# A hybrid encoder step whose down passes start with two interleaved products

## The chip, the cores and the metric

The kernel runs on one core of one Trainium2 chip. The metric is the device time of one execution in microseconds. TensorE (PE) does the matrix products, VectorE (DVE) and ScalarE (ACT) the element work, GpSimd (POOL) a few sums and some loads, and SyncE (SP) issues most loads and all stores.

## What is computed

One layer of a streaming encoder on 576 tokens (512 prompt frames and 64 sample frames), width 1024:

```
h = x + 1/2 * SwiGLU_1(RMSNorm(x))          # 1024 -> 2816 -> 1024
u = RMSNorm(h); q, k, v = split(u @ w_in)   # rotary on q and k
o = [sliding-window attention with sinks, differential attention] (u)
h = h + o @ w_out
h = h + 1/2 * SwiGLU_2(RMSNorm(h))
y = RMSNorm(h)
swiglu(x) = (silu(x @ wg) * (x @ wu)) @ wd
```

All of it is float32. The new keys and values are outputs too. The change touches only the two SwiGLU blocks, called FFN here.

## The kernel before

**Numbers in two parts.** Each operand is held as a high part (a copy rounded to a shorter float format, made by ACT) and a low part (the rest, made by DVE with a subtraction). A product of two such operands is three matmuls: high by high, high by low, low by high. Tiles are named `w_hi`, `w_lo` (weights), `c_hi`, `c_lo` (FFN input) and `h_hi`, `h_lo` (hidden activations). Making `w_lo` is what the code calls `lo_...`; making `w_hi` is `hi_...`.

**Periods.** After the first five hidden tiles of an FFN, the work goes in 28 periods, numbered p = 0 to 27. A period multiplies a 2 by 2 arrangement of blocks with seven products instead of eight (the Winograd form of Strassen's scheme), called P1, P5, P6, P2, P7, P3, P4 in the order in which PE runs them. A period of kind `st` makes one gate and one up tile of the hidden layer from the FFN input; a period of kind `sd` makes two output tiles of a down pass. The down projection is done in three passes, over the hidden tiles 0 to 7 (periods 4 to 7), 8 to 15 (periods 16 to 19) and 16 to 21 (periods 25 to 27, the first of which is called `BRIDGE`). So a down pass starts in the middle of the `st` periods, as soon as its hidden tiles are there. A product has 12 matmuls (4 k-tiles by 3), and 9 in the third pass.

**Banks.** P1, P6, P7 and P4 of a period sum up in one PSUM bank (A), P5 and P3 in another (C), P2 in a third (B). Partial sums are needed on their way, so ACT copies a bank out after P1, P5, P6 and P7 ("snapshots", `snap`, line 1436, into the tile `comb`). The next product that adds into that bank waits for the copy: P6 waits for the snapshot of P1, P3 for that of P5, P7 for that of P6, P4 for that of P7. PE waits for the weights as well: P6 and P3 need `lo_sums`, which is DVE's subtraction for two of the seven weight blocks.

**The order on the engines.** Everything is written out by hand, and every engine runs its instructions in that order; semaphores tie them. In an `st` period DVE takes the result out of the banks at the end with `take_c22` (line 1989, tile `side`) and `take_c1` (line 1998, tile `gate`, counted by the semaphore `g_out`). At the start of the next period ACT applies the silu to that `gate` (line 1364, waits for `g_out`), and only then takes that period's snapshots. `hidden` on DVE multiplies gate by up.

**Where a down pass starts.** The first period of a down pass needs the hidden tiles of the pass. Those of the last one or two are made shortly before: DVE's `pair_lo_a` (line 1898, tile `h_lo`) is the last, and PE's P1 waits for it before its last k-tile (semaphore `h_ready`).

**The last periods.** In periods 25 to 27 the output tiles are finished one by one. ACT makes the next stage's input from them (`next_hi`, line 1344, tile `u_hi`, in the first FFN only) and their squares (`next_square`, line 1564), POOL adds the squares (line 2431) and DVE makes the low part (`next_u`, line 1819). `add_first` and `add_second` on DVE (lines 2011 to 2029) add the products into the residual `res`. After the first FFN PE goes on with the projections and then with the sum over features of the squares (line 839), which waits for POOL's last addition.

Of the kernel before, what the change touches and what calls it, by code (L numbers as in the profile page):

```python
# [25 lines left out]
P = 128  # L26
# [3 lines left out]
HALF = TOK // 2  # L30
# [4 lines left out]
KF = D_FF // P  # L35
PLAIN = 5
PAIRED = 8
TAIL_FROM = 2 * PAIRED
TAIL = KF - TAIL_FROM
KH = KD // 2  # L40
# [10 lines left out]
PART = KH * P  # L51
PARTS = 7
# [41 lines left out]
def k_tiles(p):  # L94

    return TAIL // 2 if p >= BRIDGE else KH
# [77 lines left out]
def h_count(ffn, e, f):  # L174

    return len(H_EVENTS) * ffn + H_EVENTS.index((e, f)) + 1
# [5 lines left out]
def pair_slot(f, slot):  # L182

    if f < TAIL_FROM:
        return PARTS * (f % PAIRED // 2) + slot
    return (PARTS + 1) * ((f - TAIL_FROM) // 2) + slot + (slot >= B21)
# [203 lines left out]
def hybrid_step(nc, a, o):  # L390

    stack = ExitStack()
    with stack:
# [9 lines left out]
        w_hi = sb("w_hi", [P, PARTS * PART], FP32R)  # L403
# [219 lines left out]
        def side_of(p):  # L623

            return (p + 1) % 2
# [193 lines left out]
        def _(pe):  # L819
# [73 lines left out]
                else:  # L893
                    pe.wait_ge(d_second if n == P1 else d_first, sd_count(ffn, *former[1:]) + 1)

            def period_products(ffn, p):

                key = period_key(ffn, p)
                group, snaps = GROUP[key], 4 * (N_PERIODS * ffn + p)
                for n, (banks, c, slot) in enumerate(PRODUCTS):  # L900

                    pe.wait_ge(split_ready, group + {P1: 1, P5: 2, P6: 3, P2: 1, P7: 2, P3: 3, P4: 4}[n])
                    wait_period_banks(ffn, p, n)
                    if n in (P6, P7, P3, P4):

                        pe.wait_ge(snapped, snaps + {P6: 1, P3: 2, P7: 3, P4: 4}[n])
                    for k in range(k_tiles(p)):
                        if p == 0:
                            pe.wait_ge(c_ready, KH * ffn + k + 1)
                        elif key[0] == "sd" and key[3] == 0:  # L910
                            f = PAIRED * key[2] + 2 * k + 1
                            if f == KF - 1:
                                if n in (P1, P5):

                                    pe.wait_ge(h_ready, h_count(ffn, *(("E", f - 1) if n == P1 else ("A", f))))
                            elif n == P1:
                                pe.wait_ge(h_ready, max(h_count(ffn, "A", f), h_count(ffn, "B", f)))
                        if key[0] == "st":
                            x_hi, x_lo = c_hi[:, k, c, :], c_lo[:, k, c, :]
                        else:  # L920
                            at = pair_slot(PAIRED * key[2] + 2 * k, slot)
                            x_hi, x_lo = pair_hi[:, at, :], pair_lo[:, at, :]
                        col = n * PART + k * P
                        for e, (w_part, x_part) in enumerate(((w_hi, x_hi), (w_hi, x_lo), (w_lo, x_hi))):
                            m = nc.tensor.matmul(acc[:, banks[side_of(p)], 0:HALF], w_part[:, col:col + P],  # L925
                                                 x_part, start=n in (P1, P5, P2) and k == 0 and e == 0,
                                                 stop=k == k_tiles(p) - 1 and e == 2, skip_group_check=True)
                    m.then_inc(block_used, 1)

            def down_products(ffn, d, k, token_halves=(0, 1)):  # L930

# [342 lines left out]
        def _(act):  # L1274
# [227 lines left out]
            def late_period(ffn_no, p):  # L1502

                last = p == N_PERIODS - 1
                done = FINISHED[p]
                hi_a22(ffn_no, p)
                if p == BRIDGE:
                    hi_down(ffn_no, KD - 1, 0)
                    hi_down(ffn_no, KD - 1, 1)
                elif ffn_no == 0:  # L1510
                    next_hi(ffn_no, done[0])
                snap(snap_g[:, p % 2, 0, :], ffn_no, p, P1)
                if p > BRIDGE:
                    next_square(ffn_no, done[0])
                snap(snap_u[:, 1, :], ffn_no, p, P5)
                if ffn_no == 0:
                    next_hi(ffn_no, done[-1])
                snap(snap_g[:, p % 2, 1, :], ffn_no, p, P6)
                next_square(ffn_no, done[-1])
                if not last:  # L1520
                    hi_a1(ffn_no, p + 1)
                elif ffn_no == 0:
                    hi_block(("qk", 0))
                snap(snap_u[:, 0, :], ffn_no, p, P7)
                if not last:
                    hi_loaded_sums(ffn_no, p + 1)
                    hi_sums(ffn_no, p + 1)
# [22 lines left out]
            def next_hi(ffn_no, i):  # L1550

                wait_finished(ffn_no, i)
                u_hi_part(1, ORDER[i])
# [199 lines left out]
        def _(dve):  # L1753
# [278 lines left out]
            def period(ffn_no, p):  # L2032

                former = PERIODS[p - 1] if p else ("st", PLAIN - 1)
                f = former[1] if former[0] == "st" else None
                if p == 0:
                    pair_lo_b(ffn_no, PLAIN - 2)
                    lo_sums(ffn_no, p)
                    up_out(ffn_no, PLAIN - 1)
                if p >= 2 and PERIODS[p - 2][0] == "st" and PERIODS[p - 2][1] in ONE_LATER:  # L2040
                    pair_lo_a(ffn_no, PERIODS[p - 2][1])
                lo_a22(ffn_no, p)
                if f is None:
                    add_second(ffn_no, p - 1)
                else:
                    hidden(ffn_no, f)
                weight_sums(ffn_no, p + 1)
                if p == BRIDGE - 1:
                    pair_lo_e(ffn_no, KF - 2)
                    lo_down(ffn_no, KD - 2, 0)  # L2050
                    take_c22(ffn_no, p)
                    take_c1(ffn_no, p)
                    lo_down(ffn_no, KD - 2, 1)
                    lo_a1(ffn_no, p + 1)
                    hidden(ffn_no, KF - 1)
                    pair_lo_b(ffn_no, KF - 1)
                    lo_loaded_sums(ffn_no, p + 1)
                    pair_lo_a(ffn_no, KF - 1)
                    lo_sums(ffn_no, p + 1)
                    return  # L2060
                if f is not None and f % 2:
                    pair_lo_b(ffn_no, f)
                lo_a1(ffn_no, p + 1)
                lo_loaded_sums(ffn_no, p + 1)
                if f in (PAIRED - 1, TAIL_FROM - 1):
                    pair_lo_a(ffn_no, f)
                if PERIODS[p][0] == "st":
                    take_c22(ffn_no, p)
                    take_c1(ffn_no, p)
                else:  # L2070
                    for step in range(3):
                        add_first(ffn_no, p, step)
                lo_sums(ffn_no, p + 1)

            def late_period(ffn_no, p):

# [575 lines left out]
```

## Time and profile before

| what | value |
|---|---|
| median of 3 runs | 1053.2 us (1052.46 to 1053.62) |
| span of the profiled execution, first to last instruction | 1050.4 us |
| PE busy | 1034.0 us, 98% |
| DVE busy | 805.4 us, 77% |
| ACT busy | 561.3 us, 53% |
| POOL busy | 167.3 us, 16% |
| mean granted clock of PE | 0.996 of full speed |
| matmuls of the periods (line 925) | 4,578 of 7,644 |

The profile gives the span of its execution; its time as the runs count it is not given apart, and the median of the runs lies 2.8 us above the span. PE's busy time counts overlapping matmuls once, so a gap of PE shows best in the distance between the starts of two matmuls.

### The profile page before, as it was taken

How to read it: one execution, taken by the hardware profiler on the slowest of the kernel's cores; microseconds unless marked ns; L12 is line 12 of the kernel's file. 1: busy time of each engine (PE TensorE's matmuls, PEld its weight loads, DVE VectorE, ACT ScalarE, POOL GpSimd, SP SyncE). 2: the span in 40 equal slices, each digit the busy share in tenths (PEclk: the TensorE clock that was granted, in tenths of full speed). 3: DMA queues.
4: the chain of work that ended last, by engine and by line, in shares of the span. 5: the costliest groups of instructions: out<-in, count | busy, mean ns of one | idle time of the engine just before them, and what ended most of it. 6: DMA issues, size and time to landing. Idle time of an engine off the chain costs nothing. (4 is left out here: it accounts for less than half of the span.)

```text
span 1050.4 us, 19614 instructions
## 1 busy us (share of the span) xinstructions
PE 1034.0 (98%) x7644; PEld 1001.7 (95%) x7644; DVE 805.4 (77%) x1259; ACT 561.3 (53%) x971; POOL 167.3 (16%) x296
## 2 busy tenths in 40 slices
PE   9999999999999999999999999999999999999996
PEld 9999999999999999988888889999999999999995
DVE  6998777788778994377757865798877788778894
ACT  7535644665546663344335544544654566555663
POOL 0000000000000055032444202200000000000023
PEclk9999999999999999999999999999999999999998
DMA  5435666566675435120112212416656666666532
GB/s 207 128 96 155 182 158 182 154 161 168 164 180 172 123 91 201 61 95 21 51 51 71 76 41 80 121 41 169 186 148 161 169 164 168 178 151 171 161 84 90
DMA packets 38506, 137.33 MB, mean 131 GB/s; under 512 B 4688, under 2 KB 8272, under 8 KB 38288
## 3 DMA queue, kind: packets, MB, share of 16 engines
q1 hardware_dynamic: 30352, 107.52, 29.8%
q0 software_dynamic: 8064, 28.58, 16.8%
q8 instruction: 61, 1.00, 0.4%
q14 instruction: 29, 0.24, 0.1%
HBM read 131.10 MB, written 4.98 MB: 130 GB/s over the span
## 5 line engine op out<-in xcount | busy, mean ns | idle before, releaser
L1765 DVE TENSOR_TENSOR w_lo<-raw,w_hi 128x1024 fp32r<-128x1024 f32 (+4 forms) x187 | 198.9, 1066 | 109.8 <-ACT w_hi L1280 93.4
L925 PE MATMUL acc<-c_hi,w_lo 128*128 128x288 f32 x952 | 282.0, 296 | 0.0
L925 PE MATMUL acc<-c_hi,w_hi 128*128 128x288 f32 x952 | 280.9, 295 | 0.0
L925 PE MATMUL acc<-c_lo,w_hi 128*128 128x288 f32 x952 | 277.6, 292 | 0.0
L1280 ACT ACTIVATE w_hi<-raw 128x1024 fp32r<-128x1024 f32 (+4 forms) x157 | 140.6, 897 | 80.4 <-PE acc L925 57.0
L1436 ACT ACTIVATE comb<-acc 128x288 f32<-128x288 f32 x224 | 92.1, 411 | 166.9 <-PE acc L925 164.6
L925 PEld LDWEIGHTS acc<-c_lo,w_hi 128*128 128x128 f32 x952 | 180.8, 190 | 0.0
L925 PEld LDWEIGHTS acc<-c_hi,w_hi 128*128 128x128 f32 x952 | 179.1, 188 | 0.0
L925 PEld LDWEIGHTS acc<-c_hi,w_lo 128*128 128x128 f32 x952 | 178.5, 188 | 0.0
L925 PE MATMUL acc<-h_hi,w_hi 128*128 128x288 f32 x574 | 170.7, 297 | 1.9 <-DVE h_lo L1898 0.8
L925 PE MATMUL acc<-h_hi,w_lo 128*128 128x288 f32 x574 | 169.9, 296 | 0.0
L925 PE MATMUL acc<-h_lo,w_hi 128*128 128x288 f32 x574 | 167.9, 292 | 0.0
L1765 DVE TENSOR_TENSOR w_lo<-comb,w_hi 128x1024 fp32r<-128x1024 f32 (+2 forms) x86 | 101.3, 1178 | 18.2 <-ACT w_hi L1298 15.8
L925 PEld LDWEIGHTS acc<-h_hi,w_hi 128*128 128x128 f32 x574 | 107.9, 188 | 4.3 <-DVE h_lo L1898 1.7
L925 PEld LDWEIGHTS acc<-h_lo,w_hi 128*128 128x128 f32 x574 | 108.8, 190 | 0.0
L925 PEld LDWEIGHTS acc<-h_hi,w_lo 128*128 128x128 f32 x574 | 107.8, 188 | 0.0
L829 PE MATMUL acc<-h_hi,w_hi 128*128 128x288 f32 x320 | 69.3, 298 | 0.0
L829 PE MATMUL acc<-h_lo,w_hi 128*128 128x288 f32 x320 | 68.5, 295 | 0.0
L829 PE MATMUL acc<-h_hi,w_lo 128*128 128x288 f32 x320 | 68.5, 295 | 0.0
L1304 ACT ACTIVATE w_hi<-comb 128x1024 fp32r<-128x1024 f32 (+1 forms) x56 | 58.1, 1037 | 8.9 <-PE acc L925 7.5
L829 PEld LDWEIGHTS acc<-h_hi,w_hi 128*128 128x128 f32 x320 | 51.7, 188 | 0.2
L2431 POOL TENSOR_TENSOR side<-side 128x576 f32<-128x576 f32 x23 | 36.8, 1602 | 93.2 <-issue 53.0
(257 smaller groups left out, 1858.9 us busy)
## 6 DMA issues: line engine op xcount, KB each, us to landing
raw<-in_w1st SPq DMA_DIRECT2D x17, 768.0 KB, 4.3
raw<-in_w2st SPq DMA_DIRECT2D x17, 768.0 KB, 4.2
raw<-in_w_qk SPq DMA_DIRECT2D x13, 512.0 KB, 3.8
raw<-in_w1sd SPq DMA_DIRECT2D x8, 768.0 KB, 4.2
raw<-in_w2sd SPq DMA_DIRECT2D x8, 768.0 KB, 4.3
raw<-in_w1gu SPq DMA_DIRECT2D x10, 512.0 KB, 4.5
raw<-in_w2gu SPq DMA_DIRECT2D x10, 512.0 KB, 3.9
raw<-in_w1st SPq DMA_DIRECT2D x9, 512.0 KB, 5.1
```

The source lines that it names most:

```text
L829: m = nc.tensor.matmul(acc[:, bank + t, 0:HALF], w_part[:, col:col + P], x_part[:, k, t * HALF:(t + 1) * HALF], start=first and n == 0, st ...
L925: m = nc.tensor.matmul(acc[:, banks[side_of(p)], 0:HALF], w_part[:, col:col + P], x_part, start=n in (P1, P5, P2) and k == 0 and e == 0, s ...
L1280: nc.scalar.activation(cols, src, ACT.Copy).then_inc(hi_ready, 1)
L1304: nc.scalar.activation(parts_of(w_hi, P6, P3 - P6, p), w_sum[:, :, 0:width(p)], ACT.Copy).then_inc(hi_ready, 1)
L1436: nc.scalar.activation(to, acc[:, PRODUCTS[n][0][side_of(p)], 0:HALF], ACT.Copy, scale=scale).then_inc(snapped, 1)
L1765: return nc.vector.tensor_tensor(cols, src, hi.bitcast(FP32), ALU.subtract).then_inc(split_ready, 1)
L2431: nc.gpsimd.tensor_tensor(ssq[:], ssq[:], square, ALU.add).then_inc(ssq_added, 1)
```

## The change

There are three edits, all in the FFN.

**PE.** In the first period of each down pass (4, 16 and 25 of each FFN) P1 and P5 are interleaved: P1 without its last k-tile, P5 without its last two, the last of P1, the last two of P5. All other products stay whole. The loop body moved into a function of its own, `product_steps`.

**DVE.** In the period before the first two down passes (periods 3 and 15), `lo_sums` of the next period stands ahead of `take_c22` and `take_c1` instead of behind them.

**ACT.** In the last periods of the first FFN, `next_hi` stands behind a snapshot instead of ahead of it: for the first finished tile of periods 26 and 27 behind that of P1 and not ahead of it, for the last finished tile behind that of P6 and not of P5. (In periods 26 and 27 both moves apply, in the bridge the second.)

```
-            def period_products(ffn, p):
+            def product_steps(ffn, p, n, steps):
...
+                banks, c, slot = PRODUCTS[n]
+                if steps[0] == 0:
                     pe.wait_ge(split_ready, group + {P1: 1, P5: 2, P6: 3, P2: 1, P7: 2, P3: 3, P4: 4}[n])
                     wait_period_banks(ffn, p, n)
                     if n in (P6, P7, P3, P4):
                         pe.wait_ge(snapped, snaps + {P6: 1, P3: 2, P7: 3, P4: 4}[n])
...
+            def period_products(ffn, p):
+                kind, *at = PERIODS[p]
+                n_k = k_tiles(p)
+                if kind == "sd" and at[1] == 0:
+                    last = n_k - 1
+                    for n, steps in ((P1, range(last)), (P5, range(last - 1)), (P1, range(last, n_k)),
+                                     (P5, range(last - 1, n_k))):
+                        product_steps(ffn, p, n, steps)
+                    rest = range(P6, PARTS)
+                else:
+                    rest = range(PARTS)
+                for n in rest:
+                    product_steps(ffn, p, n, range(n_k))
@@ ScalarE, late_period
                 if p == BRIDGE:
                     hi_down(ffn_no, KD - 1, 0)
                     hi_down(ffn_no, KD - 1, 1)
-                elif ffn_no == 0:
-                    next_hi(ffn_no, done[0])
                 snap(snap_g[:, p % 2, 0, :], ffn_no, p, P1)
                 if p > BRIDGE:
+                    if ffn_no == 0:
+                        next_hi(ffn_no, done[0])
                     next_square(ffn_no, done[0])
                 snap(snap_u[:, 1, :], ffn_no, p, P5)
+                snap(snap_g[:, p % 2, 1, :], ffn_no, p, P6)
                 if ffn_no == 0:
                     next_hi(ffn_no, done[-1])
-                snap(snap_g[:, p % 2, 1, :], ffn_no, p, P6)
                 next_square(ffn_no, done[-1])
@@ VectorE, period
                 lo_loaded_sums(ffn_no, p + 1)
                 if f in (PAIRED - 1, TAIL_FROM - 1):
                     pair_lo_a(ffn_no, f)
+                    lo_sums(ffn_no, p + 1)
                 if PERIODS[p][0] == "st":
                     take_c22(ffn_no, p)
                     take_c1(ffn_no, p)
...
-                lo_sums(ffn_no, p + 1)
+                if f not in (PAIRED - 1, TAIL_FROM - 1):
+                    lo_sums(ffn_no, p + 1)
```

The order on DVE at the end of period 3 of the first FFN, before. Line 1898 is `pair_lo_a`, 1989 `take_c22`, 1998 `take_c1`; the first line 1765 behind them is `lo_sums` of period 4 and the second `lo_a22`.

```order
L1898 TENSOR_TENSOR h_lo<-side,h_hi 128x1440 [waits hhi_ready,q_ready]
L1989 TENSOR_TENSOR side<-comb 128x288 [waits h_ready,snapped]
L1998 TENSOR_TENSOR gate<-acc,comb 128x576 [waits h_full,block_used]
L1765 TENSOR_TENSOR w_lo<-comb,w_hi 128x2x512 [waits hi_ready]
L1765 TENSOR_TENSOR w_lo<-raw,w_hi 128x512 [waits hi_ready]
L1875 TENSOR_TENSOR side<-side,gate 128x576 [waits c21_out,h_ready,silu_done,u_out]
```

The same place after the change, where every line number of DVE is 17 higher.

```order
L1915 TENSOR_TENSOR h_lo<-side,h_hi 128x1440 [waits hhi_ready,q_ready]
L1782 TENSOR_TENSOR w_lo<-comb,w_hi 128x2x512 [waits hi_ready]
L2006 TENSOR_TENSOR side<-comb 128x288 [waits h_ready,snapped]
L2015 TENSOR_TENSOR gate<-acc,comb 128x576 [waits h_full,block_used]
L1782 TENSOR_TENSOR w_lo<-raw,w_hi 128x512 [waits hi_ready]
L1892 TENSOR_TENSOR side<-side,gate 128x576 [waits c21_out,h_ready,silu_done,u_out]
```

The subtraction into `w_lo` from `comb` went from behind the two bank sums to ahead of them; nothing else moved. ACT's order at this place is the same in both: the silu on `gate`, then the snapshots.

```order
L1445 ACTIVATE side<-acc 128x288 [waits h_full,block_used]
L1280 ACTIVATE w_hi<-raw 128x512 [waits block_used,raw_in4]
L1364 ACTIVATE gate<-gate 128x576 [waits g_out]
L1436 ACTIVATE comb<-acc 128x288 [waits block_used,g_out]
L1436 ACTIVATE comb<-acc 128x288 [waits block_used,u_out]
```

The first line 1436 is the snapshot of P1 of period 4, and it stands behind the line 1364 that waits for `g_out`.

The order on ACT in the bridge of the first FFN, before: line 1436 are snapshots (of P1, P5 and P6), 1344 is `next_hi` and 1564 `next_square`.

```order
L1320 ACTIVATE c_lo<-comb 128x256 [waits block_used,down_in]
L1436 ACTIVATE comb<-acc 128x288 [waits block_used,g_out]
L1436 ACTIVATE comb<-acc 128x288 [waits block_used,u_out]
L1344 ACTIVATE u_hi<-res,gains 128x576 [waits res_ready]
L1436 ACTIVATE comb<-acc 128x288 [waits block_used,g_out]
L1564 ACTIVATE side<-res 128x576 [waits h_ready,res_ready]
```

After the change, where ACT's numbers are 17 higher too.

```order
L1337 ACTIVATE c_lo<-comb 128x256 [waits block_used,down_in]
L1453 ACTIVATE comb<-acc 128x288 [waits block_used,g_out]
L1453 ACTIVATE comb<-acc 128x288 [waits block_used,u_out]
L1453 ACTIVATE comb<-acc 128x288 [waits block_used,g_out]
L1361 ACTIVATE u_hi<-res,gains 128x576 [waits res_ready]
L1581 ACTIVATE side<-res 128x576 [waits h_ready,res_ready]
```

The snapshot of P6 went ahead of the copy that waits for the finished tile.

## Rows read from the trace of the kernel before

**Rows 1.** The page: the span, and each engine's busy time.

```profile
span 1050.4 us, 19614 instructions
...
PE 1034.0 (98%) x7644; PEld 1001.7 (95%) x7644; DVE 805.4 (77%) x1259; ACT 561.3 (53%) x971; POOL 167.3 (16%) x296
```

**Rows 2.** PE's waits: what waited, for what: us in total, times, longest us.

```profile
PE acc L925 <- DVE h_lo L1898: 0.8, 4, 0.2
...
PE acc L925 <- ACT comb L1436: 0.8, 2, 0.4
```

**Rows 3.** The chain that ended last: start us, us, what.

```profile
767.20 129.25 PE acc L925 x975
```

**Rows 4.** Timeline, PE, first down pass of the second FFN: start us, us, engine, line, tiles.

```profile
766.70 0.29 PE L925 MATMUL acc<-h_hi,w_lo 128*128 128x288 f32 x1
...
767.20 0.40 PE L925 MATMUL acc<-h_hi,w_hi 128*128 128x288 f32 x1 [0.20 <-DVE h_lo L1898]
...
767.44 0.30 PE L925 MATMUL acc<-h_lo,w_hi 128*128 128x288 f32 x1
...
769.16 0.29 PE L925 MATMUL acc<-h_hi,w_lo 128*128 128x288 f32 x1
...
769.37 0.40 PE L925 MATMUL acc<-h_hi,w_hi 128*128 128x288 f32 x1
```

**Rows 5.** Timeline, DVE, the same stretch.

```profile
765.49 1.66 DVE L1898 TENSOR_TENSOR h_lo<-side,h_hi 128x1440 fp32r<-128x1440 f32 x1
767.06 0.45 DVE L1989 TENSOR_TENSOR side<-comb 128x288 f32<-128x288 f32 x1
767.43 0.75 DVE L1998 TENSOR_TENSOR gate<-acc,comb 128x576 f32<-128x576 f32 x1
768.10 1.21 DVE L1765 TENSOR_TENSOR w_lo<-comb,w_hi 128x1024 fp32r<-128x1024 f32 x1
769.23 0.68 DVE L1765 TENSOR_TENSOR w_lo<-raw,w_hi 128x512 fp32r<-128x512 f32 x1
```

**Rows 6.** Timeline, ACT, the same stretch.

```profile
768.22 0.69 ACT L1364 ACTIVATE gate<-gate 128x576 f32<-128x576 f32 x1 [1.07 <-DVE gate L1998]
768.81 0.39 ACT L1436 ACTIVATE comb<-acc 128x288 f32<-128x288 f32 x1
769.56 0.41 ACT L1436 ACTIVATE comb<-acc 128x288 f32<-128x288 f32 x1 [0.36 <-PE acc L925]
```

**Rows 7.** Timeline, all engines, first down pass of the first FFN.

```profile
122.64 0.40 PE L925 MATMUL acc<-h_hi,w_hi 128*128 128x288 f32 x1 [0.20 <-DVE h_lo L1898]
...
122.87 0.75 DVE L1998 TENSOR_TENSOR gate<-acc,comb 128x576 f32<-128x576 f32 x1
```

**Rows 8.** Timeline, PE and ACT, last periods of the first FFN.

```profile
364.52 0.78 ACT L1344 ACTIVATE u_hi<-res,gains 128x576 fp32r<-128x576 f32 x1 [1.09 <-DVE res L2115]
...
365.03 0.29 PE L925 MATMUL acc<-h_hi,w_lo 128*128 128x288 f32 x1
...
365.20 0.39 ACT L1436 ACTIVATE comb<-acc 128x288 f32<-128x288 f32 x1
...
365.74 0.37 PE L925 MATMUL acc<-h_hi,w_hi 128*128 128x288 f32 x1 [0.41 <-ACT comb L1436]
...
380.72 0.37 PE L925 MATMUL acc<-h_hi,w_hi 128*128 128x288 f32 x1 [0.40 <-ACT comb L1436]
```

**Rows 9.** Timeline, DVE, POOL and PE, towards the end of the first FFN.

```profile
366.07 0.75 DVE L2012 TENSOR_TENSOR res<-res,comb 128x576 f32<-128x576 f32 x1
...
374.43 1.64 POOL L2431 TENSOR_TENSOR side<-side 128x576 f32<-128x576 f32 x1 [1.02 <-ACT side L1564]
...
374.71 1.98 DVE L2012 TENSOR_TENSOR res<-res,comb 128x576 f32<-128x576 f32 x1
...
398.59 0.61 PE L839 MATMUL acc<-ones,side 128*128 128x1 f32 x4 [0.21 <-POOL side L2431]
```

**Rows 10.** Busy time by engine in a stretch: from:to, length, PE, PEld, DVE, ACT, POOL.

```profile
372.00:397.00 25.00, 24.60 (x186) 24.40 (x185) 24.82 (x29) 15.61 (x26) 10.50 (x7) 1.00 0.37 120
```

More of the change, by code:

```diff
@@ L894, in wait_period_banks @@
                     pe.wait_ge(d_second if n == P1 else d_first, sd_count(ffn, *former[1:]) + 1)
-            def period_products(ffn, p):
+            def product_steps(ffn, p, n, steps):
                 key = period_key(ffn, p)
                 group, snaps = GROUP[key], 4 * (N_PERIODS * ffn + p)
-                for n, (banks, c, slot) in enumerate(PRODUCTS):
+                banks, c, slot = PRODUCTS[n]
+                if steps[0] == 0:
                     pe.wait_ge(split_ready, group + {P1: 1, P5: 2, P6: 3, P2: 1, P7: 2, P3: 3, P4: 4}[n])
@@ L906, in period_products @@
                         pe.wait_ge(snapped, snaps + {P6: 1, P3: 2, P7: 3, P4: 4}[n])
[L907 to L927, printed above, removed]
@@ L928, in period_products @@
-                    m.then_inc(block_used, 1)
+                for k in steps:
+                    if p == 0:
+                        pe.wait_ge(c_ready, KH * ffn + k + 1)
+                    elif key[0] == "sd" and key[3] == 0 and n in (P1, P5):
+                        f = PAIRED * key[2] + 2 * k + 1
+                        if f == KF - 1:
+                            pe.wait_ge(h_ready, h_count(ffn, *(("E", f - 1) if n == P1 else ("A", f))))
+                        elif n == P1:
+                            pe.wait_ge(h_ready, max(h_count(ffn, "A", f), h_count(ffn, "B", f)))
+                    if key[0] == "st":
+                        x_hi, x_lo = c_hi[:, k, c, :], c_lo[:, k, c, :]
+                    else:
+                        at = pair_slot(PAIRED * key[2] + 2 * k, slot)
+                        x_hi, x_lo = pair_hi[:, at, :], pair_lo[:, at, :]
+                    col = n * PART + k * P
+                    for e, (w_part, x_part) in enumerate(((w_hi, x_hi), (w_hi, x_lo), (w_lo, x_hi))):
+                        m = nc.tensor.matmul(acc[:, banks[side_of(p)], 0:HALF], w_part[:, col:col + P],
+                                             x_part, start=n in (P1, P5, P2) and k == 0 and e == 0,
+                                             stop=k == k_tiles(p) - 1 and e == 2, skip_group_check=True)
@@ new lines, in product_steps @@
+                if steps[-1] == k_tiles(p) - 1:
+                    m.then_inc(block_used, 1)
+            def period_products(ffn, p):
[7 more added lines that the diff above has]
+                    rest = range(P6, PARTS)
+                else:
+                    rest = range(PARTS)
+                for n in rest:
+                    product_steps(ffn, p, n, range(n_k))
```

## The prediction

> **What bounds the kernel now.** I read the page first: PE is busy for 1034.0 of 1050.4 us [rows 1], so what PE loses is what can be won, and any delay that PE cannot make up is paid in full. The waits of PE come next, since the change moves what PE waits for. Four matmuls of the periods waited for `h_lo` and two for a snapshot in `comb` [rows 2]. The waits are short, but a wait costs more than its idle time, so the third view is the timeline of PE at these places, with the distance between starts. The chain shows what that distance is in free running: 975 matmuls in 129.25 us, 0.133 us each, with no stop from 767.20 on [rows 3]. That row says one thing more: behind the start of a down pass nothing else limits PE for 129 us, so a delay there is not made up.
>
> **A down pass's start, before.** In the second FFN the last matmul of P1's third k-tile starts at 766.70, the next one at 767.20 and the one behind it at 767.44 [rows 4]. Instead of 0.133 these distances are 0.50 and 0.24, a loss of 0.37 and 0.11: 0.48 us. The releaser is `h_lo`, which DVE makes from 765.49 on [rows 5]. There is a second, smaller loss. P5's last matmul starts at 769.16 and P6's first at 769.37 [rows 4]: 0.21, so 0.08 lost, and its restart is as long (0.40) as that of the first stall, so I add the same 0.11. Together 0.67 us at each down pass's start. The first FFN has the same picture: the restart behind `h_lo` at 122.64 and line 1998 at 122.87, 0.23 apart, as 767.20 and 767.43 are [rows 4, 5 and 7]. With the count of four [rows 2] that makes 2.7 us, and this is all that the interleaving can win.
>
> Why does P6 start at 769.37? It needs two things. One is `lo_sums`, from 768.10 for 1.21 us, so done at 769.31 [rows 5]. The other is the snapshot of P1. ACT idles for 1.07 us until `gate` is there, runs the silu at 768.22 and the snapshot of P1 at 768.81, though a product's snapshot can start 0.40 behind its last matmul (769.16 to 769.56, P5) [rows 4 and 6]. From a snapshot's start to the matmul it lets go it is 0.54 (365.20 to 365.74) [rows 8]. So the snapshot alone would allow P6 at 769.35. The two conditions end together, within 0.02 us.
>
> **Interleaving, at the first two passes.** P1's last k-tile moves behind six matmuls of P5, to 0.133 x 7 = 0.93 us behind 766.70, so 767.63. `h_lo` allowed it at 767.20: the wait is gone. P6 then would like to start 16 distances behind 766.70, at 768.82. What is late next is P6's pair of conditions.
>
> **The swap on DVE.** Behind `pair_lo_a` DVE is free at 767.06. Now `lo_sums` runs first, for 1.13 us (768.10 to 769.23, start to start), then line 1989 at 768.19 for 0.37, then line 1998 at 768.56 instead of 767.43 [rows 5]. One condition of P6, the weights, is met at 768.27, in good time. The other is not: the silu starts 0.79 behind line 1998 (767.43 to 768.22), the snapshot of P1 0.59 behind the silu (768.22 to 768.81) [rows 5 and 6], P6 0.54 behind the snapshot. 768.56 + 0.79 + 0.59 + 0.54 = 770.48. Against 768.82 that is a stall of 1.66 us, and 0.11 for the restart: 1.77 us. Before it was 0.67. Each of the four starts costs 1.10 us more: +4.4 us. P5's snapshot follows at once and P3 is 36 matmuls on; DVE's own line 1875 behind the silu slips from 769.84 to about 770.0, and nobody needs it soon. The bounds of this term: nothing less than the 1.10 by these rows unless the snapshot runs ahead of the silu, which the order excludes; 0.2 more or less at each for the latencies, so 3.6 to 5.2.
>
> **Interleaving, at the third pass.** PE shows no wait there to be won. P1's end moves back by three matmuls, 0.40 us, and 7 distances (0.93) are left to P6. The snapshot needs 0.40 to start and 0.54 to release: 0.94. I take 0.05 us for each of the two bridges, 0.1 in all; bounds 0 and 0.4 (a restart of 0.11 and as much waiting, twice).
>
> **The copies on ACT, in the first FFN.** In the bridge ACT waits 1.09 us for `res`, runs `next_hi` at 364.52 and the snapshot of P6 at 365.20. PE's starts are 365.03 and 365.74, 0.71 apart: 0.58 lost and a restart of 0.1 [rows 8]. With the snapshot ahead this stall goes, and likewise the one at 380.72 (0.40 idle, against 0.41): 1.4 us by PE's rows alone. But this is not what sets the end of the FFN. From 372 to 397 DVE is busy for 24.82 of 25.00 us [rows 10], in an order that the change leaves alone, and PE then stops at 398.59 for the last of POOL's sums of squares [rows 9], which come from tiles that DVE finishes. A PE that is 1.4 us early waits 1.4 us there. What counts is how much earlier DVE and POOL are, and for that only the copies' own shift of some tenths speaks. I take 0.2 us won. Bounds: 1.4 won if the wait at 398.59 moves with PE; 1.2 lost if the new order puts an addition of POOL in front of a DVE instruction that PE needs (line 2012 takes 0.75 us alone, and 1.98 when POOL's addition has just started at 374.43) [rows 9].
>
> The Trainium skill bears on this (page "SBUF — State Buffer", section "Who interferes with whom"): a VectorE instruction with two SBUF inputs and a GpSimd instruction that reads SBUF exclude each other for the whole instruction. The 1.98 us agree: POOL's 1.64 from 374.43 end at 376.07, and 0.62 of DVE's time lies behind. By this rule DVE's stretch is a fixed sum of its own work and POOL's eight additions, and the term would be 0; by PE's rows alone it would be -1.4.
>
> **The sum.** 4.4 + 0.1 - 0.2 = +4.3 us on the profiled span, 1050.4 to 1054.7. The median of the runs lies 2.8 us above the span, so 1053.2 + 4.3 = 1057.5 us. A change of 0.2% (2.1 us) is what a measurement of this kernel can tell from none.
>
> **The rivals.**
>
> The wait goes and nothing takes its place (faster). P6 starts at 768.82 at all four places. It decides on line 1998: for 768.82 it would have to start at 768.82 - 1.92 = 766.90, and it started at 767.43 before `lo_sums` stood ahead of it. For it: the weights, which the trace names as releaser, are early now. Against it: ACT's 1.07 us of idle time ahead of the silu, and the order. Price: -2.7 and the copies' -0.2 to -1.4: 1050.3 to 1049.1. Chance 0.06.
>
> The edits do not do what they say (same). Were the swap without effect, P6 would start at 769.37 as before, and only one of two restarts would be saved: 4 x 0.11 = 0.4, with the copies 0.6: 1052.6. It would need a silu that is not held up by line 1998. Chance 0.07.
>
> The delay is given back at the end of the first FFN. Two of the four delays, 2.2 us, come ahead of the stretch in which PE waits for DVE and POOL; if that stretch hung on transfers alone, PE would only wait less. For it: DVE's 24.82 of 25.00. Against it: DVE's work there starts from PE's products and from splits that PE's pace sets. 1057.5 - 2.2 = 1055.3. Chance 0.06.
>
> The copies collide (slower still). POOL's additions meet other DVE instructions, and one that PE needs is held for 1.2 us: 1057.5 + 0.2 + 1.2 = 1058.9. Rows 9 show that it happens to instructions there; against it, none of them stopped PE before. Chance 0.09.
>
> **How the numbers follow.** My forecast has 0.72. Its own range is 3.6 to 5.2 for the four starts, 0 to 0.4 for the bridges and -1.4 to +0.2 for the copies; not all ends meet, so 1056.0 to 1058.5. The range for 8 in 10 reaches down to where the delay is given back and up to the collision: 1054.9 to 1059.0. Slower holds the forecast and the two cases beside it, less a remainder for cases that mix: 0.85. Same 0.08, faster 0.07.
>
> **What would show it.** In the changed kernel's waits of PE, `h_lo` is gone and four waits for `comb` of about 1.3 us or more stand at P6 of periods 4 and 16, with a distance between starts near 1.8 us. On ACT the silu there has an idle time of about 2.2 us for `gate` (1.07 before), and the snapshot follows it 0.59 later. The starts at 365.74 and 380.72 lose their wait, and the one at 398.59 grows. The prediction is wrong if P6 of period 4 starts less than 3.0 us behind the last matmul of P1's third k-tile (3.78 forecast, 2.67 before), or if the sum at line 839 shows no longer wait than before.

## The result, and the profile after

| | before | after |
|---|---|---|
| median | 1053.07 us (1052.25 to 1053.62, 6 runs) | 1060.18 us (1057.04 to 1061.81, 6 runs) |
| span of the profiled execution | 1050.4 us | 1058.0 us |
| mean granted clock in it | 0.996 | 0.992 |

The ratio is 1.0066 with an interval of 1.0056 to 1.0077: slower, as forecast, but by 7.1 us where 4.3 were forecast, and outside the range (1054.9 to 1059.0). The page of the changed kernel:

```profile
span 1058.0 us, 19614 instructions
...
PE 1036.4 (98%) x7644; PEld 1004.7 (95%) x7644; DVE 805.8 (76%) x1259; ACT 561.0 (53%) x971; POOL 168.5 (16%) x296
```

Against [rows 1] PE does the same 7,644 matmuls in 2.4 us more of busy time. A wait is not counted as busy, so this is the first sign that something besides waits is in the 7.6 us between the two spans.

**The start of a down pass.** PE's waits in the changed kernel (us in total, times, longest):

```profile
PE acc L925 <- ACT comb L1453: 6.0, 4, 1.5
```

The wait for `h_lo` [rows 2] is gone and four waits for the snapshot have come. The place of [rows 4] in the timeline of PE after:

```profile
771.92 0.30 PE L925 MATMUL acc<-h_hi,w_lo 128*128 128x288 f32 x1
...
773.90 0.29 PE L925 MATMUL acc<-h_hi,w_lo 128*128 128x288 f32 x1
775.69 0.37 PE L925 MATMUL acc<-h_hi,w_hi 128*128 128x288 f32 x1 [1.49 <-ACT comb L1453]
775.90 0.29 PE L925 MATMUL acc<-h_lo,w_hi 128*128 128x288 f32 x1
```

DVE and ACT there, the places of [rows 5] and [rows 6]:

```profile
770.70 1.66 DVE L1915 TENSOR_TENSOR h_lo<-side,h_hi 128x1440 fp32r<-128x1440 f32 x1
772.28 1.22 DVE L1782 TENSOR_TENSOR w_lo<-comb,w_hi 128x1024 fp32r<-128x1024 f32 x1
773.41 0.45 DVE L2006 TENSOR_TENSOR side<-comb 128x288 f32<-128x288 f32 x1
773.78 0.75 DVE L2015 TENSOR_TENSOR gate<-acc,comb 128x576 f32<-128x576 f32 x1
```

```profile
774.57 0.68 ACT L1381 ACTIVATE gate<-gate 128x576 f32<-128x576 f32 x1 [2.20 <-DVE gate L2015]
775.16 0.69 ACT L1453 ACTIVATE comb<-acc 128x288 f32<-128x288 f32 x2
```

The reader follows the forecast's path: `lo_sums` for 1.13 us from start to start (772.28 to 773.41), `gate`, the silu 0.79 behind it, the snapshot 0.59 behind that, P6 another 0.53 later. From the last matmul of P1's third k-tile (771.92) P6 is 3.77 away; forecast was 3.78, and before it was 2.67.

**The bridge and the copies.** ACT and PE in the bridge of the first FFN after [rows 8 for before]:

```profile
366.58 0.41 ACT L1453 ACTIVATE comb<-acc 128x288 f32<-128x288 f32 x1 [0.88 <-PE acc L925]
366.89 0.77 ACT L1361 ACTIVATE u_hi<-res,gains 128x576 fp32r<-128x576 f32 x1
```

```profile
365.05 0.38 PE L925 MATMUL acc<-h_hi,w_hi 128*128 128x288 f32 x1
365.26 0.30 PE L925 MATMUL acc<-h_lo,w_hi 128*128 128x288 f32 x1
...
367.52 0.30 PE L925 MATMUL acc<-h_hi,w_hi 128*128 128x288 f32 x1
...
379.95 0.40 PE L925 MATMUL acc<-h_hi,w_hi 128*128 128x288 f32 x1 [0.35 <-DVE w_lo L1782]
...
399.64 0.53 PE L829 MATMUL acc<-u_hi,w_hi 128*128 128x288 f32 x2 [0.32 <-DVE u_lo L1836]
...
400.92 1.26 PE L839 MATMUL acc<-ones,side 128*128 128x1 f32 x10 [0.21 <-POOL side L2450]
```

The matmul that stood at 365.74 with a wait for `comb` is at 367.52 without one. But PE now waits 0.35 us for `w_lo` and 0.32 us for `u_lo`, both made by DVE, and at line 839 as long as before. The 1.4 us were waited away, ahead of line 839 and not at it. DVE itself meets POOL's additions at other places than before:

```profile
372.65 1.79 DVE L1782 TENSOR_TENSOR w_lo<-raw,w_hi 128x384 fp32r<-128x384 f32 x1
...
383.42 3.36 DVE L1836 SCALAR_TENSOR_TENSOR u_lo<-res,gains,u_hi 128x576 fp32r<-128x576 f32 x3
```

In the kernel before the first of these took 0.55 us and the three of the second 4.62. What one loses the other wins, nearly.

**What the forecast did not have.** Stretches of 2 us of the changed kernel: from:to, length, busy PE, PEld, DVE, ACT and POOL, then the granted clock, DMA share and GB/s.

```profile
402.00:404.00 2.00, 2.00 (x11) 1.99 (x12) 1.24 (x8) 1.57 (x3) 0.00 (x0) 0.67 0.18 74
404.00:406.00 2.00, 2.00 (x10) 2.00 (x10) 1.42 (x2) 0.00 (x0) 0.00 (x0) 0.50 0.00 0
406.00:408.00 2.00, 2.00 (x13) 1.79 (x13) 0.00 (x0) 0.65 (x1) 0.00 (x0) 0.98 0.74 192
636.00:638.00 2.00, 1.04 (x8) 0.81 (x7) 1.02 (x3) 1.84 (x3) 0.00 (x0) 1.00 0.00 0
638.00:640.00 2.00, 2.00 (x9) 2.00 (x10) 2.00 (x2) 0.00 (x0) 0.00 (x0) 0.55 0.00 0
640.00:642.00 2.00, 2.00 (x12) 2.00 (x11) 1.11 (x3) 1.06 (x2) 0.00 (x0) 0.60 0.80 244
```

The kernel before at the same work:

```profile
400.00:402.00 2.00, 2.00 (x16) 2.00 (x16) 1.57 (x8) 1.46 (x3) 0.00 (x0) 1.00 0.13 54
402.00:404.00 2.00, 2.00 (x14) 1.79 (x13) 1.09 (x1) 0.55 (x1) 0.00 (x0) 1.00 0.00 0
...
634.00:636.00 2.00, 1.90 (x14) 1.90 (x15) 2.00 (x3) 0.01 (x1) 0.00 (x0) 1.00 0.00 0
```

From 402 and from 638 on PE is busy all the time, but it starts 9 to 12 matmuls in 2 us where the kernel before starts 14 to 16. A clock of 0.50 is the lower of PE's two levels, 1.2 of 2.4 GHz; finer windows put the two stretches at 402.7 to 406.1 and at 638.2 to 641.6. In the timeline of the second stretch this is the distance between pairs of matmuls, first before, then after:

```profile
634.10 0.53 PE L829 MATMUL acc<-mix_hi,w_hi 128*128 128x288 f32 x2 [0.97 <-DVE mix_lo L2302]
634.47 0.43 PE L829 MATMUL acc<-mix_lo,w_hi 128*128 128x288 f32 x2
634.73 0.43 PE L829 MATMUL acc<-mix_hi,w_lo 128*128 128x288 f32 x2
```

```profile
637.98 0.69 PE L829 MATMUL acc<-mix_hi,w_hi 128*128 128x288 f32 x2 [0.96 <-DVE mix_lo L2321]
638.47 0.68 PE L829 MATMUL acc<-mix_lo,w_hi 128*128 128x288 f32 x2
638.95 0.68 PE L829 MATMUL acc<-mix_hi,w_lo 128*128 128x288 f32 x2
```

Pairs are 0.26 apart before and 0.48 after. Each such stretch costs about 1.5 us, by the account that follows.

**The account of the profiled execution**, by how much later the same matmul starts: at line 839, +2.33 (398.59 [rows 9] to 400.92), which is the two starts of the first FFN and the copies (without the copies it is +2.12, as the first experiment shows). At the end of P1's third k-tile in the second FFN, +5.22 (766.70 [rows 4] to 771.92): the 2.89 between are the two slow stretches. (Without the copies, at full clock throughout, nothing is lost between: P6 of that pass starts at 772.61, 3.24 late, which is the 2.12 and one more start.) At P6 there, +6.32 (769.37 to 775.69), so this start cost 1.10. At the end +7.6, of which another start is 1.1 and 0.2 the rest.

### The profile page after: what moved, and what is told of

Same layout as the page of the kernel before. It is cut to its first block and busy times, and to the rows that moved or that the text cites. A ratio compares the mean times of both kernels' runs of the same rounds, so it can differ in the third digit from the quotient of the medians.

```text
span 1058.0 us, 19614 instructions
## 1 busy us (share of the span) xinstructions
PE 1036.4 (98%) x7644; PEld 1004.7 (95%) x7644; DVE 805.8 (76%) x1259; ACT 561.0 (53%) x971; POOL 168.5 (16%) x296
```

## The experiments

"Whole change" is the changed kernel. Each kernel ran beside the kernel before on the same chip; that one had 1053.07 us (6 runs) beside the changed kernel's first six, 1052.63 (23) beside the four with parts of the change, 1053.02 (29) beside the repeat of the whole change and the first three with the snapshot first, and 1052.58 (20) beside the three with matmuls filled in and "the same again". These groups ran on different chips, so the ratios compare better than the medians do. The last two columns are the lowest span of any execution, and how many had a mean granted clock of 0.994 or less. That count takes in the end of the program too, where every profile has the lower level for its last 6 to 14 us, so it is not a count of slow stretches.

| kernel | median us (range, runs) | ratio (interval) | lowest span | clock ≤ 0.994 |
|---|---|---|---|---|
| before | see above | 1 | 1049.4 | 10 of 72 |
| whole change, with its repeat | 1058.82 (1056.35 to 1061.81, 11) | 1.0066 (1.0056 to 1.0077); 1.0047 (1.0034 to 1.006) | 1054.5 | 7 of 11 |
| without the copies | 1057.19 (1056.74 to 1057.87, 5) | 1.0045 (1.0033 to 1.0057) | 1054.2 | 0 of 5 |
| copies only | 1052.48 (1051.08 to 1053.89, 11) | 0.9999 (0.9991 to 1.0008) | 1049.2 | 1 of 11 |
| swap only | 1058.33 (1056.9 to 1063.54, 6) | 1.006 (1.0043 to 1.0077) | 1054.6 | 2 of 6 |
| interleaving only | 1052.48 (1051.29 to 1053.33, 11) | 0.9995 (0.9986 to 1.0003) | 1049.4 | 0 of 11 |
| snapshot first, without copies | 1051.08 (1049.29 to 1053.68, 11) | 0.998 (0.9971 to 0.999) | 1047.4 | 2 of 11 |
| the same again | 1050.08 (1049.2 to 1052.55, 8) | 0.9976 (0.9965 to 0.9987) | 1047.3 | 2 of 8 |
| snapshot first, whole change | 1052.52 (1049.8 to 1055.25, 12) | 0.9993 (0.9982 to 1.0005) | 1047.3 | 9 of 12 |
| snapshot first only | 1052.09 (1051.64 to 1054.75, 11) | 1.0001 (0.9993 to 1.001) | 1049.4 | 3 of 11 |
| whole, six matmuls more near 400 | 1056.61 (1056.11 to 1058.49, 5) | 1.0036 (1.0023 to 1.0048) | 1054.2 | 1 of 5 |
| snapshot first, whole, six more | 1050.52 (1049.57 to 1052.92, 11) | 0.9983 (0.9973 to 0.9993) | 1047.7 | 4 of 11 |
| whole, PE's stops at the starts filled | 1059.33 (1056.87 to 1061.28, 6) | 1.0056 (1.0041 to 1.007) | 1055.0 | 5 of 6 |

**Without the copies**: ACT's order in the last periods of the first FFN as before.

```
+                elif ffn_no == 0:
+                    next_hi(ffn_no, done[0])
                 snap(snap_g[:, p % 2, 0, :], ffn_no, p, P1)
                 if p > BRIDGE:
-                    if ffn_no == 0:
-                        next_hi(ffn_no, done[0])
                     next_square(ffn_no, done[0])
                 snap(snap_u[:, 1, :], ffn_no, p, P5)
-                snap(snap_g[:, p % 2, 1, :], ffn_no, p, P6)
                 if ffn_no == 0:
                     next_hi(ffn_no, done[-1])
+                snap(snap_g[:, p % 2, 1, :], ffn_no, p, P6)
```

> The change without its edit on ACT (the copies of the last periods stand as before). Known so far: the four stalls at P6 came as forecast (1.78 us between starts), and the rest of the +7 us are two short stretches in which PE's granted clock is halved, at 403 and 638 us, 1.3 to 1.5 us each. Theory A, the halved stretch near 403 comes from PE's longer stop there, which the earlier snapshots of the last periods make: without them no halved stretch near 403, runs around 1053.1 + 4.4 = 1057.5, at most one drop (near 638) in a run, so up to 1059. Theory B, the drops come with any shift of the program in time, whatever the edit: as with the whole change, around 1060 with a spread of 4 us. Theory C, ACT's edit wins its 1.4 us in the changed kernel: this one is 1.4 us slower than the whole change, 1061.5.

The four waits of 1.5 us are all there, the two for the snapshots in the last periods are back (six in all, 6.7 us), and the median is 1.6 us below that of the whole change's 11 runs. By the ratios a loss by the copies is not clear of the noise: 1.0045 here, 1.0066 and 1.0047 for the whole change, with intervals that overlap for the repeat. Line 839 starts at 400.71, 0.21 us ahead of the whole change's, and the clock stays at 1.00 behind it. So the copies, which should win a little, win nothing here.

**Copies only**: the kernel before with ACT's edit.

> The kernel before with the edit on ACT alone (copies behind the snapshots in the last periods of the first FFN). Theory A: the two waits for a snapshot in periods 25 and 27 are gone, PE comes 1 us or so earlier to the projection and stops there longer for DVE and POOL; net -0.2 us without a drop of the clock, and +1.4 us in the runs that have one near 400: 1052.9 to 1054.5. Theory B: no shift in front of the last periods, so no drop at all: 1052.9. Theory C, the gain is real: 1053.1 - 1.4 = 1051.7.

No difference. PE stands still 0.29 us for `u_lo` at 397.48 and 0.21 at line 839, which starts at 398.74 instead of 398.59: the 1.4 us are waited away before that. The slow stretch near 400 is not in this profile, although both stops are. Its mean clock is 0.993 all the same, and this is the end of the program:

```profile
1038.00:1040.00 2.00, 2.00 (x4) 1.03 (x4) 0.23 (x1) 0.74 (x2) 0.22 (x1) 0.50 0.00 0
```

The clock falls at 1038.0, 14.0 us before the last instruction. In the kernel before it falls at 1041.0, 9.4 us before the last, and in a kernel that follows below (snapshot first only) at 1043.3, 6.1 us before. The three spans are 1052.0, 1050.4 and 1049.4 us, and none of the three has a slow stretch elsewhere. So an earlier fall at the end goes with spans more than 2 us longer.

**Swap only**: the kernel before with DVE's edit.

> The kernel before with the swap on DVE alone (the weight split ahead of the two bank sums), products not interleaved. My reading: P6 starts where the snapshot behind the silu lets it, 3.78 us behind P1's third k-tile, interleaved or not. The wait for h_lo stays (0.48 us) but lies in front of the stall, so it costs nothing more: +1.1 us at each of four places, 1057.5 without drops of the clock, up to 1060 with them. Rival: the swap costs only what DVE's order costs it, some tenths, and the interleaving made the stall: 1053.1 to 1053.5.

PE at the first down pass of the first FFN with the swap alone:

```profile
122.05 0.29 PE L925 MATMUL acc<-h_hi,w_lo 128*128 128x288 f32 x1
122.55 0.40 PE L925 MATMUL acc<-h_hi,w_hi 128*128 128x288 f32 x1 [0.21 <-DVE h_lo L1898]
...
124.52 0.29 PE L925 MATMUL acc<-h_hi,w_lo 128*128 128x288 f32 x1
125.83 0.37 PE L925 MATMUL acc<-h_hi,w_hi 128*128 128x288 f32 x1 [1.02 <-ACT comb L1436]
```

From 122.05 to 125.83 it is 3.78 us, the same as with the interleaving (3.77). The swap alone carries the whole loss of the mechanism; the interleaving only moves idle time from one place to the other.

**Interleaving only**: the kernel before with PE's edit.

> The kernel before with the interleaving on PE alone; DVE and ACT as before. My reading: the wait for h_lo goes, P6 still starts at about 2.67 us behind P1's third k-tile, held by the weight split and the snapshot together, and only one restart is saved: 4 x 0.1 = 0.4 us, 1052.7. Rival: the four waits for h_lo were worth what they show, 4 x 0.48: 1051.2. Second rival: P1's later end makes its snapshot late: 1053.5 or more.

The same place:

```profile
124.08 0.29 PE L925 MATMUL acc<-h_hi,w_lo 128*128 128x288 f32 x1
124.75 0.40 PE L925 MATMUL acc<-h_hi,w_hi 128*128 128x288 f32 x1 [0.38 <-DVE w_lo L1782]
```

P1's wait is gone, and 0.67 is lost from 124.08 on by the late weights (0.54 beyond a normal distance). Either edit alone wins nothing: P6 waits for two conditions that end together, as the forecast read from [rows 5, 6 and 8].

**The whole change again.**

> The whole change once more, beside the kernels below. Without ACT's edit the runs lay at 1056.7 to 1057.9, with it at 1057.0 to 1061.8, and the profiled one had the clock halved near 403 and 638 us. Theory A, the drops come by chance and this kernel's first six runs had many of them: the median falls to about 1057.5, runs with a mean clock of 0.995 or more at 1057, those with 0.992 or less 3 us above. Theory B, ACT's edit and the delayed starts together make them (PE stops longer ahead of the sum of squares): the median stays at 1060, most runs at 0.992 or less, though each part alone has few.

1058.52 in 5 runs, where the first 6 had 1060.18. Sorted by their mean clock, the 11 executions have spans of 1054.5 and 1055.2 (clock 0.996) up to 1058.0 to 1058.3 (0.992) and 1059.2 (0.990). The profiled one has a slow stretch near 404 too, none at 638, and one more from 24 on. So the slow stretches are not fixed parts of this kernel. How many an execution gets, and when its clock falls at the end, go with its place within 5 us.

**The snapshot first.** In the first period of the first two down passes ACT takes the snapshot of P1 ahead of the silu. This takes away what the late `gate` holds up. Three kernels: on the whole change without the copies, on the whole change, and on the kernel before.

```
                 hi_a22(ffn_no, p)
+                starts = PERIODS[p][0] == "sd" and PERIODS[p][2] == 0
+                if starts:
+                    snap(snap_g[:, p % 2, 0, :], ffn_no, p, P1)
                 if p and f is not None:
                     silu(ffn_no, f)
-                snap(snap_g[:, p % 2, 0, :], ffn_no, p, P1)
+                if not starts:
+                    snap(snap_g[:, p % 2, 0, :], ffn_no, p, P1)
```

> Interleaving and swap as in the change, ACT's last periods as before, and at the first period of the first two down passes ACT takes the snapshot of P1 ahead of the silu. My reading: what held P6 was the silu's wait for the bank sum, in front of the snapshot; the snapshot can start at 768.3 (in the times of the second FFN's first pass) and lets P6 go at 768.83, the weights are ready at 768.27, so no stall is left at these four places: 4 x 0.67 = 2.7 us less than before, 1049.9. Rival: the snapshot was not it (DVE's line 1998 or another wait holds P6): 1057 as without this edit.

> The whole change, ACT's edit in the last periods too, and the snapshot of P1 ahead of the silu as in the kernel beside it. My reading: the same 1049.9 or up to 0.2 less, since what ACT's edit wins is waited away at the end of the first FFN. Rival: with PE on time the edit brings its 1.4 us: 1048.5. If ACT's edit brings drops of the clock by itself, 1 to 3 us more than the kernel beside it, and a wider spread.

> The kernel before with nothing but the snapshot of P1 ahead of the silu at the same four places. My reading: P6 has two conditions that ended within 0.02 us; with the snapshot early the weight split still ends at 769.31, so nothing is won: 1052.6. Rival: the snapshot alone was the bound: 4 x 0.19 = 0.8 us less, 1051.8.

PE at the first start, snapshot first without the copies:

```profile
124.17 0.29 PE L925 MATMUL acc<-h_hi,w_lo 128*128 128x288 f32 x1
124.31 0.38 PE L925 MATMUL acc<-h_hi,w_hi 128*128 128x288 f32 x1
124.53 0.29 PE L925 MATMUL acc<-h_lo,w_hi 128*128 128x288 f32 x1
```

P6 starts 0.14 behind P5, and a restart of 0.09 is left. The lowest span goes from 1054.2 to 1047.4, 6.8 us for one exchanged pair of instructions, and 2.0 below the kernel before. On the kernel before the same exchange does nothing, since `h_lo` and the weights still hold PE. By these waits all three are needed: interleaving for `h_lo`, the swap for the weights, this one for the snapshot. That the snapshot needs the other two both is read from the rows; with only one of them it was not run.

With the copies added it should have been as fast. Its lowest span is (1047.3), but its median is 1.4 us higher, and 9 of its 12 executions have a clock of 0.994 or less, where 4 of 19 have it without the copies. Its profile near 400:

```profile
398.00:400.00 2.00, 2.00 (x15) 1.97 (x15) 0.58 (x4) 1.13 (x3) 0.00 (x0) 0.85 0.44 172
400.00:402.00 2.00, 2.00 (x10) 2.00 (x9) 2.00 (x5) 0.44 (x1) 0.00 (x0) 0.50 0.00 0
```

**Six matmuls more near 400.** Three are put ahead of the last k-tile of the first projection tile and three ahead of the sum (line 839). They write into a bank that is free there; their output is not used.

```
+            def fill(col, count):
+                for i in range(count):
+                    nc.tensor.matmul(acc[:, 7, 0:HALF], w_hi[:, col:col + P], u_hi[:, ORDER[0], 0:HALF],
+                                     start=True, stop=True)
...
+                if b == 0 and k == KD - 1:
+                    fill(split_base(("qk", 0)), 3)
                 m = feature_products(tile_bank(b), split_base(("qk", b)), d, u_hi, u_lo, d, k == 0, k == KD - 1)
...
                     if b == 0 and k == KD - 1:
+                        fill(split_base(("qk", 0)), 3)
                         token_sums(1, TOK_SUM_BANK)
```

> The whole change, and PE's two stops ahead of the sum over features after the first FFN (line 839) are filled: three matmuls of 288 columns ahead of the last k-tile of the first projection tile, three more ahead of the sum, into a bank that is free there; their output is not used. The work is late by the same amount as in the whole change. Theory 'stops' (PE's short stops just ahead of line 839 are what is followed by the stretch at half the clock near 402 us, whole change 1058.5 to 1060.2): the granted clock stays at 1.0 from 395 to 410 and 1.4 us come back, span 1054.5 to 1056.5, median near 1057.3. Rival 'place in time' (the stretch hangs on when the stops come, or on nothing in PE's work there): the stretch stays in the profiled execution and the median stays at 1058.5 to 1060. Rival 'cost of the filling': six matmuls that are not covered by waiting add 0.1 to 0.3 us.

> The same filling on the whole change with the snapshot of P1 ahead of the silu, which ran at 1052.5 with a halved stretch near 400 us in the profiled execution and a mean granted clock of 0.994 or less in 9 of its 12 executions. Theory 'stops': the stretch near 400 is gone, mean clock 0.995 or more in most executions, median 1050.6 to 1051.2, as the version without ACT's copies. Rival 'place in time': 1052.3 to 1052.7, and the clock as before.

PE in the first of the two (the matmuls of line 1042 are the added ones):

```profile
399.46 0.67 PE L1042 MATMUL acc<-u_hi,w_hi 128*128 128x288 f32 x3 [0.29 <-DVE u_lo L1844]
...
400.77 0.56 PE L1042 MATMUL acc<-u_hi,w_hi 128*128 128x288 f32 x3
401.16 1.15 PE L839 MATMUL acc<-ones,side 128*128 128x1 f32 x10
```

The edit did less than its expectation said. The first three stand behind the wait for `u_lo` and not ahead of it, so that stop is still there (0.29 us). What is gone is the stop ahead of the sum: 401.16 has no idle time before it. In this profile the stretch that had 0.67 and 0.50 in the whole change has

```profile
402.00:404.00 2.00, 2.00 (x16) 1.97 (x17) 1.10 (x7) 1.57 (x3) 0.00 (x0) 1.00 0.05 20
404.00:406.00 2.00, 2.00 (x14) 1.79 (x14) 1.55 (x2) 0.08 (x1) 0.00 (x0) 1.00 0.00 0
```

And the second, whose twin without the six had 0.85 and 0.50:

```profile
398.00:400.00 2.00, 2.00 (x19) 1.97 (x18) 0.40 (x3) 0.94 (x3) 0.00 (x0) 1.00 0.24 92
400.00:402.00 2.00, 2.00 (x16) 1.90 (x15) 2.00 (x6) 0.63 (x1) 0.00 (x0) 1.00 0.00 0
```

Six matmuls more, and the medians are 2.2 us lower (1058.82 to 1056.61) and 2.0 us lower (1052.52 to 1050.52). Some of that is the chip: against the kernel before beside each, the six take it from +7.1 and +5.5 to +4.0, and from -0.5 to -2.1, and the intervals of the ratios overlap (1.0034 to 1.006 with 1.0023 to 1.0048, 0.9982 to 1.0005 with 0.9973 to 0.9993). Counted together, 16 of 23 executions had a low clock without the six and 5 of 16 with them. The second kernel's profiled execution is one of the five: at 1.00 near 400, its clock falls some 14 us before the end, and its mean is 0.993 by that alone.

**PE's stops at the four starts filled**, with twelve matmuls between P5 and P6 into a free bank, output not used.

```
                     rest = range(P6, PARTS)
+                    if p != BRIDGE:
+                        col, at = P5 * PART, pair_slot(PAIRED * at[0], PRODUCTS[P5][2])
+                        for i in range(12):
+                            nc.tensor.matmul(acc[:, 7, 0:HALF], w_hi[:, col:col + P], pair_hi[:, at, :],
+                                             start=True, stop=True, skip_group_check=True)
```

> The whole change, and the stop of 1.66 us ahead of P6 at the four starts of the first two down passes is filled with twelve matmuls of 288 columns into a free bank (12 x 0.133 = 1.6 us), output not used. P6 still starts when the snapshot allows it. Theory 'delay': the time is set by the late snapshot, so the distance before P6 is now 13 matmuls long and the median stays within 0.5 us of the whole change (1058 to 1060), less 0.1 at each place for the restart. Rival 'the long stops cost clock': if the four stops of 1.5 us are what the later stretches at half the clock follow, these go, and the median falls to 1056.8 or less. Rival 'the delay is hidden somewhere': below 1054.

PE at the first start:

```profile
124.24 1.75 PE L945 MATMUL acc<-h_hi,w_hi 128*128 128x288 f32 x12
125.90 0.37 PE L925 MATMUL acc<-h_hi,w_hi 128*128 128x288 f32 x1
```

Twelve matmuls for nothing, and the median (1059.33) is 0.5 us above the whole change's (1058.82), its ratio (1.0056) between that kernel's two. P6 starts at 125.90, where it started at 126.03 behind the idle stop. So the stop ahead of P6 is a wait and not work of PE. The slow stretches from 402 and from 638 on are in this profile too (0.64 and 0.50, 0.52 and 0.62), so idle time at the long stops far ahead is not what they need.

## Why the prediction was right in kind and wrong in size

**The four starts: right.** Forecast 1.10 us each by way of `gate`, silu and snapshot; the trace shows 1.10 at the third, and taking the snapshot out from behind the silu takes the loss away. Forecast +4.4 for all; without the copies, and at full clock until its last 8 us, the lowest span is 4.8 above that of the kernel before (1054.2 to 1049.4).

**The bridges: right.** The forecast took 0.05 us each; the first shows a distance of 0.21 instead of 0.13 (365.05 to 365.26), 0.08 lost.

**The copies: right in sum, wrong in one reading.** They win nothing alone (ratio 0.9999, forecast −0.2 us). No row stood behind the 0.2; line 839 starts 0.15 us later by the copies alone (398.59 to 398.74) and 0.21 later in the changed kernel (400.71 to 400.92), inside the forecast's bounds. The text named the sum at line 839 as the place where PE would wait longer and made it a test. It waits 0.21 there as before; PE loses the time at `w_lo` and `u_lo`, earlier. By its own test the forecast would have been called wrong while its claim held: the test should have been the start of line 839, not its wait.

**The step that failed: the sum.** "The sum is made on the profiled span" took over that execution's clock with it. The kernel before ran at 1.00 until its last 10 us, and the sum had no term for PE's clock, neither in the likeliest value nor in the bounds. What the runs showed in its place is two stretches at 0.50 of full clock, which in the profiled execution measured 2.9 us of 7.6; the rest, 4.7, is near the 4.3 of the sum. Nor did a rival hold it: "the copies collide" gave 1058.9, near the measured time, by POOL's additions holding DVE. They do hold it at new places (1.79 us for 0.55 at 372.65), but free it at others, and line 839 starts 0.21 us later and not 1.2. Over all 11 executions the median is 1058.82, 1.3 us above the forecast and inside its range. Some 0.4 of these are the copies (0.21 later for 0.2 earlier), so the clock's share there is, as an estimate, 1 us or less, and the 1060.18 of the first six has some chance in it.

**The other rivals.** "The wait goes and nothing takes its place" was tied to the right condition, a `gate` that does not hold the snapshot. With the snapshot taken out from behind it the medians are 1051.08 and 1050.08, where the rival said 1050.3 to 1049.1. "The swap is without effect" fell with the swap alone (1.006). "The delay is given back" fell with the start of line 839, late by all of 2.33 us.

**What brings the slow stretches: open, with a lead.** Near 400 they stand in four of the five profiles with ACT's copies and nothing filled in there (whole change, its repeat, snapshot first with the copies, stops at the starts filled; not in copies only). They stand in none of the seven without the copies, where the profile marks no stop for `u_lo`, and in neither of the two with six matmuls more, where it does not stop ahead of line 839. The time alone does not divide them: line 839 starts at 400.92 and 397.58 in two with the stretch, and at 400.94 (swap only) and 397.49 (snapshot first, without copies) in two without. So what PE does there seems to count, but each profile is of one execution. The page "TensorE: Matmul & The Clock Gate" of the Trainium skill, section "What's actually happening", ties the clock to how busy PE has been shortly before; the direction agrees. But the stops do not decide alone: copies only has both of them at 397.48 and 398.74 and keeps 1.00, and the kernel before keeps 1.00 behind a stop of 0.97 us at 634.10 where the changed one, behind 0.96 us, has 0.50. Why the same stops are followed by the lower level in one execution and not in another stays open, and so does what the second stretch has to do with the change. At 638 nothing was tried; it comes where that matmul starts at 637.98 and 637.86 (stops at the starts filled) and not where it starts at 639.38 (the repeat) or 636.25 (without the copies), so there the place in time is not ruled out.

**A better version.** Interleaving, swap and snapshot first, without the copies, ran twice: 1051.08 and 1050.08 us, ratios 0.998 and 0.9976, both intervals below 1, some 2 us better than the kernel before and some 8 better than the changed one. With the copies and the six matmuls it is as good (0.9983) and no better.

## What to carry to other kernels

An instruction that a wait needs may stand behind one that has nothing to do with it, on another engine: when you move work, walk every condition of the waiting instruction back through each in-order queue, and when two conditions end together expect nothing from curing one. Ask what stands behind the moved one too: 1.13 us put ahead of `gate` came out at P6 as 1.10 us, four times. And in a kernel in which PE is busy for 98% of the span, a few short stops close to each other can be followed by a stretch at the lower clock that costs more than they do; look at the granted clock by stretch, the end of the program included, and compare medians of many executions together with their lowest spans, since the two answer different questions.

## What the runs showed of the hardware that was not expected

- After stops of 0.3 and 0.2 us within 1.3 us (399.64 and 400.92), PE ran at 0.50 from 402.7 to 406.1 while busy all the time, and lost about 1.5 us. Stops of 0.32 and 0.96 us (635.18 and 637.98) were followed by the same from 638.2 to 641.6.
- A matmul released from a wait is followed by the next after 0.21 to 0.24 us instead of 0.13, even where it started only 0.01 to 0.02 us late and the profile marks no idle time (365.05 to 365.26, 124.31 to 124.53): about 0.1 us for each wait that ends late, however short.
- The same program spreads over 5 us (1056.35 to 1061.81) with the mean granted clock, 0.996 to 0.990, while its lowest spans repeat to 0.7 us (1055.2 and 1054.5).
- At the end of the program the clock falls 6.1 us (snapshot first only) to 14.0 us (copies only) before the last instruction, and the spans of the two differ by 2.6 us though neither has a slow stretch elsewhere.
